# Three 64-byte steps in the SBUF layout of a two-model transformer kernel

## The chip, the core and the metric

The kernel runs on one core of a Trainium2 chip. The metric is the device time of one execution in microseconds (us). Within 0.5% is what a measurement of this kernel can hardly tell from no change.

## What is computed

A sequence of 256 positions with 1,024 features passes through two models of two layers each, all in float32. A layer of the first model is a feed-forward block, a mixer and a second feed-forward block, with a norm at the end:

```python
for l in range(DEPTH):
    x = x + 0.5 * swiglu_ffn(rmsnorm(x, ffn1_norm[l]), ffn1_w_up[l], ffn1_w_down[l])
    x = x + mixer(rmsnorm(x, mix_norm[l]), w_in[l], ...)
    x = x + 0.5 * swiglu_ffn(rmsnorm(x, ffn2_norm[l]), ffn2_w_up[l], ffn2_w_down[l])
    x = rmsnorm(x, final_norm[l])
```

The mixer projects its input to values, a gated convolution input, queries and keys, and gates; it runs dilated window attention and a convolution of 31 taps over the sequence, projects both, gates them, and projects the sum out. A layer of the second model has a mixer of a Fourier transform and windowed attention, and one feed-forward block with a convolution of three taps. The feed-forward width is 2,816 everywhere.

## The kernel before

**Precision in three products.** Every weight matrix is split into a high part (float32 rounded to the float32r format) and a low part, and so is every activation. A product is three matmuls into the same PSUM bank: high weights by high activations (L437), high weights by low activations (L438), low weights by high activations (L439). Each has 128 x 128 weights (stationary) and 256 columns of activations (moving). In the profile's names, `bank<-h_lo,hi` is a matmul whose moving operand is `h_lo` and whose weights are a tile of `hi`.

```python
    mm(out, w_hi, a_hi, start=start, stop=False, skip_group_check=True)
    mm(out, w_hi, a_lo, start=False, stop=False, skip_group_check=True)
    return mm(out, w_lo, a_hi, start=False, stop=True, skip_group_check=True)
```

**Weight stream.** Weights come in chunks of 128 x 2048 (16 tiles) into `raw`, which has three slots. SyncE issues the loads in the order of the program, ScalarE copies `raw` to `hi` (L1059), VectorE subtracts to get `lo` (L1570), and TensorE uses the chunk in 48 matmuls. All orders are written out by hand; no scheduler moves anything.

**Moving operands by stage.** The feed-forward blocks stream `n_hi` and `n_lo` (the scaled input) against the up weights, `hid_hi` and `hid_lo` against the down weights, and `last_hi` and `last_lo` in the last down chunk alone. The mixer of the first model streams `h_hi` and `h_lo`, its normed input, through 8 chunks of the gated convolution input (two tiles of 128 outputs by 8 tiles of features each), 12 chunks of queries and keys, and 8 chunks of gates; then `yt` and `s` through the projections of attention and convolution; then `h_hi` and `h_lo` again, which now hold the mix, through the output projection. The second model uses `n`, `f` and `g`, and `h` in its output projection. `x` and `sq` hold the residual and a scratch copy of it.

**Beside the matmuls.** In the stage of queries and keys VectorE also turns the heads (L1734, L1736), scales them (L1744) and works off the taps of the convolution (`cv`, L1771), a fixed number of taps behind each chunk.

**Layout.** `sb()` hands out SBUF addresses upward from `state["at"]`, rounded up to 64 bytes, except where an address is given; those are offsets from four marks (`at_m`, `at_a` with `at_v` and `at_u` above it, and `at_t`). The first address is 16,512. Byte addresses within a partition:

| tiles | address before | remainder by 128 |
|---|---|---|
| `raw`, `hi`, `lo` (slots of 8,192 bytes, tiles of 512) | 16,512; 41,088; 65,664 | 0 |
| `x`, `h_hi`, `h_lo`, `sq` (slices of 1,024) | 90,240; 98,432; 106,624; 114,816 | 0 |
| `const` and the masks | 123,008; 129,664 | 0 |
| `s_hi`, `f_hi`, `qk` (from `at_a`) | 144,704 | 64 |
| `hid_hi` (from `at_v`) | 169,280 | 64 |
| `n_hi`, `yt_hi`, `g_hi` (from `at_u`); `n_lo` | 181,568; 189,760 | 64 |
| `cv`, `gate` | 190,720; 198,912 | 0 |
| `zt`, `p_sb`, `sgm`, `last_hi` (from `at_t`) | 215,296 | 0 |

Of the kernel before, what the change touches and what calls it, by code (L numbers as in the profile page):

```python
# [233 lines left out]
def build(nc, d):  # L234
# [5 lines left out]
    state = {"at": -(-nc.sbuf_base // 64) * 64}  # L240

    def sb(name, shape, dt, at=None):
        size = int(np.prod(shape[1:])) * 4
        if at is None:
            at = state["at"]
            state["at"] += -(-size // 64) * 64
        return nc.alloc_sbuf_tensor_at(name, shape, dt, offset=at)

    raw = sb("raw", [P, SLOTS, CW], F32)
    hi = sb("hi", [P, SLOTS, CW], F32R)  # L250
    lo = sb("lo", [P, SLOTS, CW], F32R)
    x = sb("x", [P, KT, S], F32)
    h_hi = sb("h_hi", [P, KT, S], F32R)
    h_lo = sb("h_lo", [P, KT, S], F32R)
    sq = sb("sq", [P, KT, S], F32)
    const = sb("const", [P, C["mask1"]], F32)
    eps = const[:, C["eps"]:C["eps"] + 1]
    at_m = state["at"]
# [33 lines left out]
    gate = sb("gate", [P, 16, S], F32)  # L292
    bv = sb("bv", [P, GROUPS * 512], F32, at_u + (KT * UPW + KT * S) * 4)
    spread = sb("spread", [P, 2 * ROWS * HD], F32, at_u + (KT * UPW + KT * S) * 4 + 10240)
    at_t = state["at"]
    z = sb("z", [P, 2, S], F32)
    zsq = sb("zsq", [P, 2, S], F32)
# [2143 lines left out]
```

## Time and profile before

| | |
|---|---|
| median of the runs | 2016.39 us |
| lowest and highest of 3 | 2011.72 and 2020.76 us |
| profiled execution, its own time | 2009.35 us |
| span of its trace | 2007.5 us |
| TensorE busy | 1945.0 us (97%) |
| VectorE, ScalarE busy | 1493.7 us, 1078.1 us |
| mean granted TensorE clock | 0.992 |

Matmuls overlap in the pipeline: one has a duration of about 0.28 us in the trace, but the next starts about 0.12 us after it. So TensorE's pace is not read from durations or from the busy share, but from how many matmuls fit into a stretch in which it never stops. The rows of the trace stand below the change.

### The profile page before, as it was taken

Reading aid. Unit: us, or ns where it says so; the run is one execution under the profiler, and the core shown is the slowest. Engines: PE = TensorE matmul, PEld = TensorE weight load, DVE = VectorE, ACT = ScalarE, POOL = GpSimd, SP = SyncE. Lnnn points to the kernel's source line nnn. Section 1 sums busy time; section 2 is a strip of 40 time slices with the busy share of each in tenths; the row PEclk is TensorE's granted clock in tenths of the full one; section 3 lists DMA queues with packets and bytes.
Section 4 is the critical chain, followed back from the end, with each engine's and each line's share of the span. In section 5 each row is a group of like instructions: output and inputs, shape, how many; then the busy total and the mean of one; then the engine's idle time right before and its main releaser. Section 6 shows DMA issues by size and latency. Waiting matters only on the chain.

```text
span 2007.5 us, 39036 instructions
## 1 busy us (share of the span) xinstructions
PE 1945.0 (97%) x15906; PEld 1873.5 (93%) x15906; DVE 1493.7 (74%) x2183; ACT 1078.1 (54%) x1358; POOL 31.4 (2%) x40
## 2 busy tenths in 40 slices
PE   7999999999999999999998999999999999999998
PEld 6999999799999999999987999999889999889998
DVE  6555889987755576568899787555778777878776
ACT  5444566566544444445665765444565555565554
POOL 0000011000000000000100000000000000000000
PEclk9999999999999999999999999999999999999999
DMA  6555589534655445555985256554335554334553
GB/s 244 204 184 214 189 245 263 151 98 137 226 201 182 176 147 188 191 218 189 269 243 148 86 170 219 188 188 161 114 111 184 188 188 167 128 136 161 195 190 135
DMA packets 61001, 362.26 MB, mean 180 GB/s; under 512 B 7904, under 2 KB 8160, under 8 KB 24160
## 3 DMA queue, kind: packets, MB, share of 16 engines
q1 hardware_dynamic: 54704, 339.37, 47.9%
q0 software_dynamic: 5184, 18.88, 5.4%
q10 hardware_dynamic: 1008, 2.51, 0.3%
q8 instruction: 78, 1.28, 0.3%
q14 instruction: 27, 0.22, 0.0%
HBM read 353.39 MB, written 1.05 MB: 177 GB/s over the span
## 4 chain that ended last, share of the span: by engine, by line
PE 78%; DVE 15%; ACT 4%; DMA 2%; issue 1%; DVEq 0%; ACTq 0%; SPq 0%
PE bank L437 24%; PE bank L438 24%; PE bank L439 24%; DVE lo L1570 5%; DVE cv L1771 3%; ACT hi L1059 2%; DMA raw<-in_w 1%; DVE zt L1734 1%; PE bank L642 1%; DVE n_lo L1574 1%; PE bank L615 1%; PE bank L628 1%; DMA x<-in_x 1%; DVE qk L1744 1%; PE bank L600 0%
## 5 line engine op out<-in xcount | busy, mean ns | idle before, releaser
L1570 DVE TENSOR_TENSOR lo<-raw,hi 128x2048 fp32r<-128x2048 f32 (+1 forms) x336 | 676.5, 2014 | 216.6 <-ACT hi L1059 216.2
L437 PE MATMUL bank<-n_hi,hi 128*128 128x256 f32 x2256 | 637.3, 283 | 29.9 <-DVE lo L1798 12.6
L1059 ACT ACTIVATE hi<-raw 128x2048 fp32r<-128x2048 f32 (+1 forms) x336 | 598.3, 1783 | 105.1 <-PE bank L439 86.9
L438 PE MATMUL bank<-n_lo,hi 128*128 128x256 f32 x2256 | 631.1, 280 | 0.0
L439 PE MATMUL bank<-n_hi,lo 128*128 128x256 f32 x2256 | 631.0, 280 | 0.0
L437 PEld LDWEIGHTS bank<-n_hi,hi 128*128 128x128 f32 x2256 | 429.6, 190 | 36.0 <-DVE lo L1798 12.6
L438 PEld LDWEIGHTS bank<-n_lo,hi 128*128 128x128 f32 x2256 | 426.8, 189 | 1.2 <-issue 1.0
L439 PEld LDWEIGHTS bank<-n_hi,lo 128*128 128x128 f32 x2256 | 427.9, 190 | 0.0
L437 PE MATMUL bank<-h_hi,hi 128*128 128x256 f32 x1152 | 335.7, 291 | 4.8 <-DVE h_lo L1574 4.8
L438 PE MATMUL bank<-h_lo,hi 128*128 128x256 f32 x1152 | 326.9, 284 | 0.0
L439 PE MATMUL bank<-h_hi,lo 128*128 128x256 f32 x1152 | 326.6, 284 | 0.0
L437 PE MATMUL bank<-hid_hi,hi 128*128 128x256 f32 x960 | 267.6, 279 | 0.6 <-DVE lo L1570 0.6
L438 PE MATMUL bank<-hid_lo,hi 128*128 128x256 f32 x960 | 267.4, 279 | 0.0
L439 PE MATMUL bank<-hid_hi,lo 128*128 128x256 f32 x960 | 267.4, 279 | 0.0
L437 PEld LDWEIGHTS bank<-h_hi,hi 128*128 128x128 f32 x1152 | 221.6, 192 | 17.5 <-issue 12.5
L438 PEld LDWEIGHTS bank<-h_lo,hi 128*128 128x128 f32 x1152 | 221.9, 193 | 0.6
L439 PEld LDWEIGHTS bank<-h_hi,lo 128*128 128x128 f32 x1152 | 221.9, 193 | 0.0
L1108 ACT ACTIVATE silu_t<-up_t 128x256 f32<-128x256 f32 x88 | 36.8, 418 | 299.6 <-DVE up_t L1625 299.6
L1771 DVE SCALAR_TENSOR_TENSOR cv<-upad,prm,cv 128x256 f32<-128x256 f32 x480 | 195.2, 476 | 0.0
L437 PEld LDWEIGHTS bank<-hid_hi,hi 128*128 128x128 f32 x960 | 181.6, 189 | 1.0 <-DVE lo L1570 1.0
L439 PEld LDWEIGHTS bank<-hid_hi,lo 128*128 128x128 f32 x960 | 180.9, 188 | 0.0
L438 PEld LDWEIGHTS bank<-hid_lo,hi 128*128 128x128 f32 x960 | 180.2, 188 | 0.0
(243 smaller groups left out, 2291.5 us busy)
## 6 DMA issues: line engine op xcount, KB each, us to landing
raw<-in_w SPq DMA_DIRECT2D x286, 1024.0 KB, 4.8
raw<-in_w SPq DMA_DIRECT2D x53, 512.0 KB, 4.0
lo<-in_w POOLq DMA_DIRECT2D x36, 512.0 KB, 8.2
zt<-zt SPq DMA_DIRECT2D x96, 64.0 KB, 5.8
bv<-in_bv SPq DMA_DIRECT2D x2, 768.0 KB, 6.1
spread<-in_spread SPq DMA_DIRECT2D x2, 768.0 KB, 8.0
x<-in_x ACTq DMA_DIRECT2D x4, 256.0 KB, 10.3
out_x<-sq SPq DMA_DIRECT2D x1, 1024.0 KB, 3.9
```

Source lines behind the costliest of these rows:

```text
L437: mm(out, w_hi, a_hi, start=start, stop=False, skip_group_check=True)
L438: mm(out, w_hi, a_lo, start=False, stop=False, skip_group_check=True)
L439: return mm(out, w_lo, a_hi, start=False, stop=True, skip_group_check=True)
L615: last = mm(bank[3 + e][:, at:at + n], qk[r, 4 * g + hp, qt * P:(qt + 1) * P], qk[r, 12 + 4 * g + hp, cols], start=(g == 0), stop=True, sk ...
L628: last = nc.tensor.transpose(bank[5 + e][:, b * P:(b + 1) * P], p_sb[:, e, b * P:(b + 1) * P], ident)
L642: last = mm(bank[Y_BANK][e * HD:(e + 1) * HD, qt * P:(qt + 1) * P], v_sb[:, kt, v:v + HD], pt_sb[:, e, b, :], start=(b == 0), stop=(b == 3 ...
L1059: fn(hi[:, s, 0:w], raw[:, s, 0:w], ACT.Copy).then_inc(sem["hi"], 1)
L1108: fn(silu_t[:, u, :], gate_of[:, u, 0, :], ACT.Silu).then_inc(sem["silu"], 1)
L1570: v.tensor_tensor(lo[:, s, 0:w], raw[:, s, 0:w], hi[:, s, 0:w].bitcast(F32), ALU.subtract)\
L1574: return v.tensor_tensor(out, full, high.bitcast(F32), ALU.subtract).then_inc(sem[name], 1)
L1734: link(v.tensor_tensor(both, both, turns, ALU.mult))
L1771: ins = v.scalar_tensor_tensor(cv[:, t, :], src, w, cv[:, t, :], ALU.mult, ALU.add)
```

## The change

Three lines are added, each of which moves the mark from which the following tiles get their addresses by 64 bytes.

```diff
     lo = sb("lo", [P, SLOTS, CW], F32R)
+    state["at"] += 64
     x = sb("x", [P, KT, S], F32)
     h_hi = sb("h_hi", [P, KT, S], F32R)
     h_lo = sb("h_lo", [P, KT, S], F32R)
     sq = sb("sq", [P, KT, S], F32)
+    state["at"] += 64
     const = sb("const", [P, C["mask1"]], F32)
...
     spread = sb("spread", [P, 2 * ROWS * HD], F32, at_u + (KT * UPW + KT * S) * 4 + 10240)
+    state["at"] += 64
     at_t = state["at"]
     z = sb("z", [P, 2, S], F32)
```

`raw`, `hi` and `lo` keep their addresses. `x`, `h_hi`, `h_lo` and `sq` move up by 64 bytes, to 90,304 and so on, a remainder by 128 of 64 where it was 0. Everything from `const` to `spread` moves up by 128 bytes, so its remainder stays. `zt`, `p_sb`, `sgm`, `last_hi` and `last_lo` and what else stands behind `at_t` moves up by 192 bytes, to a remainder of 64 where it was 0. With the three lines in, the five engines have the same instructions in the same order, with the same shapes and the same waits; only base addresses differ.

## Rows read from the trace of the kernel before

**Rows 1.** The page: busy time by engine, and shares of the last-ending chain by engine.

```profile
PE 1945.0 (97%) x15906; PEld 1873.5 (93%) x15906; DVE 1493.7 (74%) x2183; ACT 1078.1 (54%) x1358; POOL 31.4 (2%) x40
PE 78%; DVE 15%; ACT 4%; DMA 2%; issue 1%; DVEq 0%; ACTq 0%; SPq 0%
```

**Rows 2.** Costliest groups by form: busy us, mean ns, by name of moving operand.

```profile
L438 PE MATMUL bank<-n_lo,hi 128*128 128x256 f32 x2256 | 631.1, 280 | 0.0
L438 PE MATMUL bank<-h_lo,hi 128*128 128x256 f32 x1152 | 326.9, 284 | 0.0
L438 PE MATMUL bank<-s_lo,hi 128*128 128x256 f32 x128 | 35.3, 276 | 0.0
L438 PE MATMUL bank<-last_lo,hi 128*128 128x256 f32 x96 | 28.6, 298 | 0.0
```

**Rows 3.** Stretches: length, each engine's busy time and instructions, clock, DMA.

```profile
core 0: us, PE busy (x) PEld busy (x) DVE busy (x) ACT busy (x) POOL busy (x), PEclk, DMA share, GB/s
229.00:277.00 48.00, 48.00 (x402) 48.00 (x402) 39.47 (x68) 24.01 (x21) 1.87 (x2) 1.00 0.62 195
473.00:493.00 20.00, 20.00 (x179) 20.00 (x178) 17.93 (x25) 10.76 (x14) 0.00 (x0) 1.00 0.62 202
27.00:197.00 170.00, 170.00 (x1446) 170.00 (x1445) 101.51 (x97) 73.54 (x76) 0.00 (x0) 1.00 0.56 200
728.00:892.00 164.00, 164.00 (x1449) 164.00 (x1449) 100.69 (x96) 73.41 (x75) 0.00 (x0) 1.00 0.56 202
1549.00:1690.00 141.00, 141.00 (x1246) 141.00 (x1246) 110.38 (x150) 80.73 (x97) 0.00 (x0) 1.00 0.54 191
199.00:204.00 5.00, 5.00 (x44) 5.00 (x43) 4.93 (x9) 3.78 (x5) 0.00 (x0) 1.00 0.40 129
894.00:899.00 5.00, 5.00 (x45) 5.00 (x44) 4.93 (x8) 3.15 (x4) 0.00 (x0) 1.00 0.33 92
```

**Rows 4.** Groups in 229:277 (h_lo) and 473:493 (s_lo): matmuls and weight loads.

```profile
L438 PE MATMUL bank<-h_lo,hi 128*128 128x256 f32 x134 | 37.9, 283 | 0.0
L438 PEld LDWEIGHTS bank<-h_lo,hi 128*128 128x128 f32 x134 | 25.7, 192 | 0.0
...
L438 PE MATMUL bank<-s_lo,hi 128*128 128x256 f32 x60 | 16.6, 276 | 0.0
L438 PEld LDWEIGHTS bank<-s_lo,hi 128*128 128x128 f32 x60 | 11.3, 188 | 0.0
```

**Rows 5.** Weight loads in 93:141, same columns as rows 4.

```profile
L439 PEld LDWEIGHTS bank<-n_hi,lo 128*128 128x128 f32 x92 | 17.7, 192 | 0.0
L437 PEld LDWEIGHTS bank<-n_hi,hi 128*128 128x128 f32 x91 | 17.1, 188 | 0.0
```

**Rows 6.** Matmuls of h_lo in 228:286, 286:319, 390:457 and 1490:1509.

```profile
L438 PE MATMUL bank<-h_lo,hi 128*128 128x256 f32 x160 | 45.3, 283 | 0.0
...
L438 PE MATMUL bank<-h_lo,hi 128*128 128x256 f32 x80 | 22.6, 283 | 0.0
...
L438 PE MATMUL bank<-h_lo,hi 128*128 128x256 f32 x98 | 28.0, 285 | 0.0
...
L438 PE MATMUL bank<-h_lo,hi 128*128 128x256 f32 x48 | 14.3, 298 | 0.0
```

**Rows 7.** Chain that ended last by line: 286:319, 319:370, 390:457, 493:519.

```profile
by line: PE bank L437 32.0%; PE bank L438 29.1%; PE bank L439 29.0%; PE bank L578 8.8%; ACT zt L1169 1.7%; issue 0.1%
...
by line: DVE cv L1771 34.2%; DVE lo L1570 20.0%; DVE zt L1734 15.7%; DVE qk L1744 7.7%; issue 6.2%; ACT hi L1059 3.5%; DVE rstd L1886 3.3%; DVE qk L1736 3.0%; ACT L1175 2.5%; ACT zgsq L1178 1.4%; DVE cv L1768 1.3%; ACT zt L1169 1.2%; ACT st
...
by line: PE bank L437 21.0%; PE bank L438 17.8%; PE bank L439 17.7%; PE bank L615 10.0%; PE bank L642 9.8%; PE bank L628 9.7%; PE bank L600 7.0%; PE bank L715 5.4%; ACT pt_sb L1197 1.6%; issue 0.1%
...
by line: DMA raw<-in_w 49.5%; DVE lo L1570 23.0%; ACT hi L1059 19.3%; issue 3.8%; DVE t L1968 3.1%; DVE sq L1971 2.7%; DVE h_lo L1574 2.7%; ACT h_hi L1326 2.5%; DVE sq L1604 2.4%; ACT xsq L1091 2.4%; DVE x L1642 2.3%; DVE t L1966 2.3%; PE b
```

**Rows 8.** Two more stretches, columns as in rows 3.

```profile
228.00:286.00 58.00, 58.00 (x484) 57.79 (x484) 48.27 (x85) 31.11 (x29) 3.60 (x4) 1.00 0.67 205
...
319.00:370.00 51.00, 49.62 (x351) 41.85 (x349) 49.21 (x83) 30.16 (x39) 4.32 (x5) 1.00 0.87 242
```

## The prediction

> **What bounds the kernel now.** First the page: TensorE is busy for 97% of the span and has 78% of the chain that ended last, VectorE 15% [rows 1]. So the pace of the matmul stream is the time, except where VectorE or the weight stream holds it up. Second the costliest groups: matmuls of one shape, one instruction and one kind of weights, have four mean durations, by the name of the moving operand: 276 ns with `s_lo`, 280 with `n_lo`, 284 with `h_lo`, 298 with `last_lo` [rows 2]. The last two are the operands whose remainder by 128 equals that of the weights in `hi` and `lo`; `s` and `n` stand at 64.
>
> Third the pace itself, from stretches in which TensorE never stops. A stretch also counts the matmuls that reach over its edges, so I divide its length plus one duration by its count. From 229 to 277 us, all `h`: (48,000 + 283) / 402 = 120.1 ns from start to start. From 473 to 493, all `s`: (20,000 + 276) / 179 = 113.3 ns. The feed-forward blocks (`n` and `hid`) have two paces. From 27 to 197: 170,281 / 1446 = 117.8 ns; from 728 to 892: 164,276 / 1449 = 113.4 ns; from 1549 to 1690: 141,276 / 1246 = 113.4 ns [rows 3]. Of the six blocks three are like the first (the stretches 529:699 and 1222:1392 have the same count) and three like the others (1845:1986 too). These are the same chunks of code at the same addresses, so a block falls into one of two paces, and keeps it to its end. `last` has 5,281 / 44 = 120.0 ns in one block and 5,281 / 45 = 117.4 ns in another [rows 3]; this count is coarse.
>
> Fourth, what is longer in the slow pace. With `s` a matmul has 276 ns and its neighbouring weight load 188; with `h` 283 and 192 [rows 4]. In a slow feed-forward block one of the three loads, that of the low tile, has 192 ns and the others 188 [rows 5]. I read this as two readers of SBUF that meet: the stream of moving columns and the load of the next tile. With equal remainders they meet at every matmul; 64 bytes apart they meet never or in part, by how the two happen to be placed in time when the stream starts. The durations show that both wait; that the remainder by 128 is what counts is my inference from which names are slow. `last`, whose address has the weights' remainder by 128 but not by 256 (0 against 128), is slow as well, so a remainder by 256 fits worse.
>
> **The change part by part.** No instruction is added, removed or reordered.
>
> *First step: `h` from remainder 0 to 64.* The `h` stream then stands to the weights as `n`, `hid`, `s` and `yt` do now. Its pace goes from 120.1 to 113.3 (6.8 ns less) or to 117.8 (2.3 ns less). By the six feed-forward blocks the chance is one half each; the `s` stretch is fast, and so I take 60% fast: 0.6 x 6.8 + 0.4 x 2.3 = 5.0 ns per matmul.
>
> Which `h` matmuls count? Each row of the groups by stretch stands for one of the three products, so times three. In 228:286 (gated convolution input and the first two chunks of queries and keys) 160 x 3 = 480; TensorE never stops there, VectorE is busy for 48.27 of 58 us and so has some 9.7 us to come forward [rows 6, 8]. In 286:319 80 x 3 = 240, and the chain runs through TensorE [rows 6, 7]. In 319:370 the chain is VectorE's: taps 34.2%, `lo` 20.0%, turning 15.7% [rows 7], with VectorE busy for 49.21 of 51 us [rows 8]; a faster matmul there buys nothing of its own, but the stage starts earlier by what was won before, since VectorE's idle time ahead of it is larger than the 720 x 6.8 = 4.9 us that it could be at most. In 390:457 (gates) 98 x 3 = 294 on a chain of TensorE [rows 6, 7]. In 493:519 (output projection) the chain goes through the weight loads (49.5%), `lo` and `hi` [rows 7]: its 192 matmuls count for 0, at most 192 x 6.8 = 1.3 us. That is 480 + 240 + 294 = 1,014 per layer, 2,028 for both. The output projection of the second model has 48 x 3 = 144 in 1490:1509 [rows 6], 288 for its two layers. Sum 2,316 x 5.0 ns = 11.6 us. Bounds: all slow 2,316 x 2.3 = 5.3 us; all fast 2,316 x 6.8 = 15.7, with the two output projections 18.4 us.
>
> *Third step: `last` from 0 to 64.* Six blocks of 48 make 288 matmuls. From a mean of (120.0 + 117.4) / 2 = 118.7 to 0.6 x 113.3 + 0.4 x 117.8 = 115.1 is 3.6 ns: 1.0 us, between 0 and 288 x 6.8 = 2.0.
>
> *`x`, `sq`, `zt`, `p_sb` and `sgm` at other remainders.* These are VectorE's, ScalarE's and the transfers'. The trace doesn't show them at other addresses. VectorE's nearest rows are the 51 us of 319:370, where turning has 15.7% of the chain [rows 7]: 1% either way on those 8 us is 0.1 us per layer. I take 0, and keep 0.5 us either way.
>
> *Second step: `n`, `hid`, `s` and the rest by 128 bytes.* Their remainder by 128 stays. I take 0. If the remainder counts by 256 after all, their relation to the weights changes from 64 below to 64 above. A gain from it can't exceed what the three slow blocks would give, (170,281 - 1446 x 113.4) ns = 6.3 us each; the loss is the rival below.
>
> Sum: 11.6 + 1.0 = 12.6 us. The profiled execution took 2009.35 us, so its like comes to 1996.8 us. The median of the runs shown is 2016.39, which is 7.0 us above it: about the price of one feed-forward block more in the slow pace. Against it the forecast is 2016.4 - 12.6 = 2003.8, **2004 us**.
>
> **A rule that speaks against it.** The rows show a matmul 7 ns and its weight load 4 ns longer with `h` than with `s` [rows 4]. The Trainium skill, "TensorE: Matmul & The Clock Gate", section "Step-by-step: what each phase is for", says that TensorE has two independent read ports of SBUF, one for the moving operand and one for the weights, and that "Loading the next tile's weights doesn't steal SBUF read bandwidth from the running matmul". By that rule the addresses cannot matter to the matmuls and the sum would be 0, 2016.4 us. The trace does not agree with it for the pace of `h`; what it leaves open is whether the address is the cause.
>
> **The rivals.**
> *No effect* (chance 0.12): the pace of `h` has another cause than its address. For it: between the stages chunk lengths, PSUM banks and VectorE's load differ too. Against it: `h` has 283 to 285 ns in three stages that differ in just these ways [rows 6]. It gives 2016 us. This is also the case that the change doesn't do what it should.
> *Always the partial meeting* (0.18): `h` falls into the pace of 117.8 ns. Then 5.3 us and little from `last`: 2011 us.
> *The feed-forward blocks go slow* (0.12, the other side): the move by 128 bytes, or the other arrival times at a block's start, put the fast blocks into the pace of 117.8 ns. The price is 4.4 ns a matmul, 1449 x 4.4 = 6.4 us for the block at 728 and 1246 x 4.4 = 5.5 us for each of the two late ones [rows 3], together 17.4 us. For it: which pace a block gets is decided at its start by times that this change moves. Against it: three of six are fast now, and nothing in their own addresses by 128 changes. With `h` in the slow pace as well it gives 2016.4 + 17.4 - 5.3 = 2028.5 us. It decides when more than two blocks flip and none flips back, since two cost 11.9 us and the forecast gains 12.6.
> *The forecast* (0.58).
>
> **How the numbers follow.** The forecast's own range is 18.4 + 2.0 = 20.4 us at most and 5.3 at least, so 1996 to 2011; a feed-forward block that falls out otherwise moves either end by 6.3. The range for 8 in 10 leaves out a block flipped on top of an all-fast case below, and most of the slow rival above: 1993 to 2017, which takes in no effect. What counts as faster is under 2006.3, which needs 10.1 us of the 12.6: the forecast and hardly any rival, 0.57. Within 0.5%, up to 2026.5: no effect, the partial meeting and single flips, 0.33. Slower: 0.10.
>
> **What would show it.** Right: the same stretch of `h` has about 425 matmuls in 48 us instead of 402, with 276 and 188 ns, or about 410 with 281; the stage of queries and keys is as long as before between its VectorE instructions but starts 1.5 to 5 us earlier; `last` falls below 281 ns in its unstalled middle. Wrong: `h` still at 283 and 192 ns (the address is not it), or `n` and `hid` at a third pace (the 128 bytes matter). The total is wrong with the mechanism right if the number of slow feed-forward blocks is not three, since one is worth half of the whole gain.

## The result and the profile after

The changed kernel has a median of 2020.53 us (20 runs, 2008.95 to 2026.47); the kernel before, run beside it, 2015.63 us (20 runs, 2009.52 to 2020.76). The ratio is 1.0024, 95% interval 1.0013 to 1.0034: about 4.9 us slower (2.6 to 6.9). The forecast was 2004 and its range ended at 2017. The profiled execution after took 2020.89 us, with a span of 2019.1 us; the one before took 2009.35 us.

First the page after, with the busy time by engine and the chain that ended last, as in [rows 1]. Three lines are added above them, so L437, L438 and L439 of before are L440, L441 and L442 here.

```profile
PE 1958.1 (97%) x15906; PEld 1886.1 (93%) x15906; DVE 1494.3 (74%) x2183; ACT 1079.0 (53%) x1358; POOL 31.4 (2%) x40
...
PE 79%; DVE 15%; ACT 3%; DMA 1%; issue 1%; DVEq 0%; ACTq 0%; SPq 0%
```

TensorE has 13 us more of busy time and the other engines have what they had: a change of pace in the main, not a new wait. The groups by form, as in [rows 2]:

```profile
L441 PE MATMUL bank<-n_lo,hi 128*128 128x256 f32 x2256 | 633.5, 281 | 0.0
...
L441 PE MATMUL bank<-h_lo,hi 128*128 128x256 f32 x1152 | 322.4, 280 | 0.0
...
L441 PE MATMUL bank<-s_lo,hi 128*128 128x256 f32 x128 | 35.7, 279 | 0.0
...
L441 PE MATMUL bank<-last_lo,hi 128*128 128x256 f32 x96 | 27.4, 285 | 0.0
```

`h_lo` fell from 284 to 280 ns and `last_lo` from 298 to 285, as meant. But `s_lo` rose from 276 to 279, and `n_lo` from 280 to 281, over 2,256 instructions. The pace shows more. The same stretches as in [rows 3], with their columns:

```profile
229.00:277.00 48.00, 48.00 (x410) 48.00 (x409) 40.12 (x69) 24.66 (x22) 1.88 (x2) 1.00 0.62 198
473.00:493.00 20.00, 20.00 (x172) 20.00 (x171) 18.06 (x26) 8.51 (x10) 0.00 (x0) 1.00 0.63 199
27.00:197.00 170.00, 170.00 (x1445) 170.00 (x1445) 101.51 (x97) 73.61 (x75) 0.00 (x0) 1.00 0.56 201
728.00:892.00 164.00, 164.00 (x1395) 164.00 (x1394) 97.27 (x90) 70.38 (x71) 0.00 (x0) 1.00 0.55 195
1549.00:1690.00 141.00, 141.00 (x1200) 141.00 (x1199) 107.52 (x146) 78.51 (x94) 0.00 (x0) 1.00 0.53 191
199.00:204.00 5.00, 5.00 (x45) 5.00 (x44) 4.93 (x9) 3.80 (x5) 0.00 (x0) 1.00 0.46 149
...
1500.00:1512.00 12.00, 12.00 (x108) 12.00 (x108) 10.11 (x16) 5.35 (x7) 0.00 (x0) 1.00 0.63 215
```

With (length + one duration) / count: `h` has 48,280 / 410 = 117.8 ns (120.1 before). `s` has 20,279 / 172 = 117.9 (113.3 before). The first feed-forward block has 117.8 as before, but the stretches of the third and the fifth have 164,281 / 1395 = 117.8 and 141,281 / 1200 = 117.7, where they had 113.4. `last` has 45 in its 5 us in the first block, where it had 44. So the two paces that the prediction read are both still there, but after the change all six feed-forward blocks, `yt`, `s` and the long stretches of `h` in the first model are in the slower one. The faster one is left in a few single chunks of `h` and in one of the two output projections of the second model (the last row, `h` at the same address: 12,276 / 108 = 113.7).

The matmuls of `h` in 229:277, as in [rows 4], with one of the three weight loads (the other two have 188 and 187 ns):

```profile
L441 PE MATMUL bank<-h_lo,hi 128*128 128x256 f32 x137 | 38.4, 280 | 0.0
...
L440 PEld LDWEIGHTS bank<-h_hi,hi 128*128 128x128 f32 x137 | 25.8, 188 | 0.0
```

The load fell from 192 to 188 ns and the matmul from 283 to 280. The weights did not move, so the duration of their load goes by the place of the moving operand. The pace is that of the partial meeting, but the durations are different from those that the prediction read for it: in the slow blocks of the kernel before one of the three loads has 192 ns and the matmuls have 281 [rows 5], while here no load has more than 188 and the matmuls have 279 or 280.

What `h` gained is seen in when the next stage starts. The matmuls of `yt_hi` (64 instructions, shortest/median/longest duration in ns, first and last start in us) in a second profile of the kernel before, and in the changed kernel:

```profile
L437 PE MATMUL bank<-yt_hi,hi x64: 276/276/473, 459.8 to 1169.8; 128*128 128x256 f32 x64
...
L440 PE MATMUL bank<-yt_hi,hi x64: 280/280/470, 457.6 to 1167.4; 128*128 128x256 f32 x64
```

The stage of `yt` starts 2.2 us earlier and runs with 280 ns instead of 276. Counted from the first matmul of `h`, which starts at 228.3 us here and at 227.8 there, it comes after 229.3 us; so it does in a second profile of the changed kernel. In three profiles with `h` at 0 (the two of before, and e1 below) it comes after 232.0 to 233.0: 2.7 to 3.7 us are won in the first layer. In the second layer it comes after 229.9 and 231.2 us, against 230.6 to 232.1, about 1 us. By its last start 2.4 us are left of this in the profile shown, and in the second profile of the changed kernel (1170.4) nothing: `yt` and `s` have given back a part, and the rest differs from one execution to the next.

The chain by line in 319:370, as in [rows 7], is still VectorE's, with turning at 15.7% in both: the new addresses of `zt`, `p_sb` and `sgm` cost nothing that this view shows. Ahead of it, in 286:319, the chain was TensorE's before [rows 7]; in the changed kernel, the second line below, it is now that of the turning of the heads (its transfer into `zt`, and VectorE).

```profile
by line: DVE cv L1774 41.2%; DVE lo L1573 19.8%; DVE zt L1737 15.7%; DVE qk L1747 7.7%; issue 5.4%; DVE qk L1739 4.3%; PE bank L618 3.6%; DVE rstd L1889 3.3%; DVE cv L1771 1.3%; DVEq L1744 0.0%
...
by line: DMA zt<-zt 31.9%; DVE cv L1774 21.6%; DVE zt L1737 10.7%; DVE lo L1573 6.9%; PE bank L442 5.6%; PE bank L440 5.1%; PE bank L441 5.1%; SPq L374 5.1%; DVE qk L1739 4.2%; ACT zt L1172 3.1%; issue 0.7%
```

### The profile page after: what moved, and what is told of

It is laid out like the page before. It is cut to its first block, busy times and chain, and to the rows that moved or that the text cites. A ratio compares the mean times of both kernels' runs of the same rounds, so it can differ in the third digit from the quotient of the medians.

```text
span 2019.1 us, 39036 instructions
## 1 busy us (share of the span) xinstructions
PE 1958.1 (97%) x15906; PEld 1886.1 (93%) x15906; DVE 1494.3 (74%) x2183; ACT 1079.0 (53%) x1358; POOL 31.4 (2%) x40
## 4 chain that ended last, share of the span: by engine, by line
PE 79%; DVE 15%; ACT 3%; DMA 1%; issue 1%; DVEq 0%; ACTq 0%; SPq 0%
PE bank L440 25%; PE bank L441 24%; PE bank L442 24%; DVE lo L1573 4%; DVE cv L1774 3%; ACT hi L1062 2%; DVE zt L1737 1%; PE bank L618 1%; PE bank L645 1%; DVE n_lo L1577 1%; PE bank L631 1%; DMA x<-in_x 1%; DMA zt<-zt 1%; DVE qk L1747 1%; DVE sq L1607 0%
## 5 line engine op out<-in xcount | busy, mean ns | idle before, releaser
L440 PE MATMUL bank<-n_hi,hi 128*128 128x256 f32 x2256 | 639.2, 283 | 29.7 <-DVE lo L1801 12.5
L442 PE MATMUL bank<-n_hi,lo 128*128 128x256 f32 x2256 | 633.5, 281 | 0.0
L441 PE MATMUL bank<-n_lo,hi 128*128 128x256 f32 x2256 | 633.5, 281 | 0.0
L440 PEld LDWEIGHTS bank<-n_hi,hi 128*128 128x128 f32 x2256 | 426.6, 189 | 35.5 <-DVE lo L1801 12.5
L441 PEld LDWEIGHTS bank<-n_lo,hi 128*128 128x128 f32 x2256 | 427.2, 189 | 1.2 <-issue 1.0
L442 PEld LDWEIGHTS bank<-n_hi,lo 128*128 128x128 f32 x2256 | 426.6, 189 | 0.0
L440 PE MATMUL bank<-h_hi,hi 128*128 128x256 f32 x1152 | 331.2, 288 | 4.1 <-DVE h_lo L1577 3.9
L441 PE MATMUL bank<-h_lo,hi 128*128 128x256 f32 x1152 | 322.4, 280 | 0.0
L442 PE MATMUL bank<-h_hi,lo 128*128 128x256 f32 x1152 | 322.0, 280 | 0.0
L440 PE MATMUL bank<-hid_hi,hi 128*128 128x256 f32 x960 | 268.2, 279 | 0.3 <-DVE lo L1573 0.3
L442 PE MATMUL bank<-hid_hi,lo 128*128 128x256 f32 x960 | 268.3, 279 | 0.0
L441 PE MATMUL bank<-hid_lo,hi 128*128 128x256 f32 x960 | 268.2, 279 | 0.0
L440 PEld LDWEIGHTS bank<-h_hi,hi 128*128 128x128 f32 x1152 | 217.2, 189 | 16.9 <-issue 13.8
L441 PEld LDWEIGHTS bank<-h_lo,hi 128*128 128x128 f32 x1152 | 217.2, 189 | 0.5
L442 PEld LDWEIGHTS bank<-h_hi,lo 128*128 128x128 f32 x1152 | 217.3, 189 | 0.0
L440 PEld LDWEIGHTS bank<-hid_hi,hi 128*128 128x128 f32 x960 | 180.0, 187 | 0.8 <-DVE lo L1573 0.8
L441 PEld LDWEIGHTS bank<-hid_lo,hi 128*128 128x128 f32 x960 | 180.2, 188 | 0.0
L442 PEld LDWEIGHTS bank<-hid_hi,lo 128*128 128x128 f32 x960 | 180.0, 188 | 0.0
```

## The experiments

In the prediction the remainder by 128 bytes of a moving operand decided how it meets the weights. By the result a rival theory is due: **by 256** (A), in which 64 above the weights and 64 below them (192 above) are different places. Its rival is **history** (B): the address counts by 128 only, and what a stage draws depends on when, and behind what, its stream starts. The table has for each kernel the bytes added ahead of `x`, `const` and `at_t`, and where the moving operands then stand above the weights by 256.

| kernel | added | `h` | `n` `hid` `s` `yt` | `last` | median (runs) | before beside it | ratio [95%] |
|---|---|---|---|---|---|---|---|
| before | 0/0/0 | 0 | 192 | 128 | | | |
| after | 64/64/64 | 64 | 64 | 64 | 2020.53 (20) | 2015.63 | 1.0024 [1.0013, 1.0034] |
| e1 | 0/128/0 | 0 | 64 | 0 | 2026.25 (5) | 2015.69 | 1.0056 [1.0037, 1.0074] |
| e2 | 64/192/0 | 64 | 192 | 128 | 2012.34 (10) | 2015.69 | 0.9991 [0.9977, 1.0004] |
| e3 | 192/64/0 | 192 | 192 | 128 | 2007.29 (10) | 2015.69 | 0.9962 [0.9946, 0.9978] |
| e4 | 32/0/0 | 32 | 224 | 160 | 2029.55 (4) | 2015.69 | 1.0070 [1.0050, 1.0091] |
| e5 | 224/0/0 | 224 | 160 | 96 | 2032.74 (8) | 2013.25 | 1.0089 [1.0062, 1.0116] |
| e6 | 96/0/0 | 96 | 32 | 224 | 2019.53 (8) | 2013.25 | 1.0024 [0.9999, 1.0049] |
| e7 | 64/0/0 | 64 | 0 | 192 | 2043.75 (2) | 2013.25 | 1.0115 [1.0061, 1.0170] |
| e9 | 192/64/64 | 192 | 192 | 192 | 2005.37 (7) | 2016.88 | 0.9941 [0.9921, 0.9961] |
| e12, as e9 | 192/64/64 | 192 | 192 | 192 | 2009.03 (10) | 2015.72 | 0.9972 [0.9947, 0.9998] |
| e10 | 32/64/64 | 32 | 32 | 32 | 2013.87 (10) | 2016.88 | 0.9981 [0.9966, 0.9996] |

All rows below are stretches with the columns of [rows 3] in which TensorE never stops (in 474:490 of e12 the weight loads pause for 0.12 us). 231:279 is `h` in the gated convolution input, 474:490 is `s`, and 60:190, 560:690, 760:890, 1260:1390, 1570:1680 and 1870:1980 lie in the six feed-forward blocks. In 48 us a pace of 120 ns has 402 matmuls, 117.8 ns has 410 and 113.4 ns has 425; in 130 us they are 1086, 1106 and 1149; in 110 us the last two are 936 and 973; in 16 us 138 and 144.

**The second step alone (e1).**

```diff
     sq = sb("sq", [P, KT, S], F32)
+    state["at"] += 128
     const = sb("const", [P, C["mask1"]], F32)
```

> x, h_hi, h_lo and sq stay at their old addresses; everything from const on moves up by 128 bytes. By 256, h then stands at 0 to the weights and n, hid, s, yt at 64 above them, where before they were 64 below; last stands at 0. Theory A (the remainder by 256 counts: 64 above is the slow pace, 64 below either): h stays at 120.1 ns, but s, yt and all six feed-forward blocks run at 117.8 ns, as in the changed kernel; the time is 1 to 1.01 of before (about +15 us against the profiled execution). Theory B (what streamed before counts: the h stream at remainder 0 sets what follows into the fast pace): s and yt at 113.3 ns, three or so of six blocks fast, and a time as before.

```profile
231.00:279.00 48.00, 48.00 (x402) 48.00 (x402) 40.09 (x71) 23.05 (x21) 2.33 (x3) 1.00 0.67 211
474.00:490.00 16.00, 16.00 (x138) 16.00 (x137) 14.34 (x20) 8.09 (x9) 0.00 (x0) 1.00 0.66 198
...
1570.00:1680.00 110.00, 110.00 (x936) 110.00 (x935) 80.11 (x111) 58.40 (x70) 0.00 (x0) 1.00 0.53 189
1870.00:1980.00 110.00, 110.00 (x973) 110.00 (x973) 84.61 (x115) 61.87 (x75) 0.00 (x0) 1.00 0.54 191
```

The ratio gives 11.3 us more (7.5 to 14.9). `h` stays at 402, as its address does. `s` has 138 and block 5 has 936, where both were fast, and only block 6 draws the fast pace. This is A: 128 bytes, which leave every remainder by 128 alone, cost more than the whole change. The line moves `last` and VectorE's tiles behind `const` too, but the loss is seen in the pace of `s` and of a late block, in stretches where TensorE never stops.

**`h` moved by 64, the rest by 256 (e2), and `h` by 192, the rest by 256 (e3).** In both, `n`, `hid`, `s` and `yt` keep their place above the weights.

```diff
     lo = sb("lo", [P, SLOTS, CW], F32R)
+    state["at"] += 64
...
     sq = sb("sq", [P, KT, S], F32)
+    state["at"] += 192
```

> x, h_hi, h_lo and sq move up by 64 bytes and everything from const on by 256, so that n, hid, s, yt keep their remainder by 256 (64 below the weights) and h stands 64 above. Theory A: h mostly 117.8 ns as in the changed kernel, s and yt and about half of the feed-forward blocks at 113.3, last as before near 119; 8 us less than before. Theory B (there is no stream at remainder 0 left ahead of s): s, yt and all blocks at 117.8 ns, 5 us more than before.

```profile
231.00:279.00 48.00, 48.00 (x410) 48.00 (x409) 41.15 (x73) 23.43 (x21) 2.73 (x3) 1.00 0.68 216
474.00:490.00 16.00, 16.00 (x139) 16.00 (x138) 14.70 (x21) 7.99 (x9) 0.00 (x0) 1.00 0.62 198
...
1570.00:1680.00 110.00, 110.00 (x937) 110.00 (x936) 81.47 (x110) 59.67 (x72) 0.00 (x0) 1.00 0.51 176
1870.00:1980.00 110.00, 110.00 (x973) 110.00 (x972) 86.71 (x115) 62.28 (x75) 0.00 (x0) 1.00 0.53 188
...
1178.00:1194.00 16.00, 16.00 (x138) 16.00 (x137) 13.96 (x20) 7.09 (x8) 0.00 (x0) 1.00 0.58 179
```

`h` has the 410 of the changed kernel. The ratio gives -1.8 us (-4.6 to +0.8), so the loss of e1 is gone when the rest stays at 192. But `s` has 139, the slow pace, at the place where it was fast before, in the second layer too (the last row, where `s` in e3 has 143), and one late block is slow. That is not in A; it is what B says. The same edit with 192 and 64 is e3:

> x, h_hi, h_lo and sq move up by 192 bytes and everything from const on by 256: h, n, hid, s and yt all stand 64 below the weights by 256. Theory A: h at 113.3 in part of its stages, the blocks half fast as before; 8 to 15 us less than before. Theory B: as the changed kernel, nearly all at 117.8 ns and 5 us more than before, since nothing at remainder 0 is left.

```profile
231.00:279.00 48.00, 48.00 (x410) 48.00 (x409) 41.20 (x74) 23.38 (x22) 2.73 (x3) 1.00 0.67 217
474.00:490.00 16.00, 16.00 (x144) 16.00 (x143) 14.48 (x21) 8.05 (x9) 0.00 (x0) 1.00 0.63 198
...
1570.00:1680.00 110.00, 110.00 (x973) 110.00 (x972) 87.54 (x117) 62.58 (x76) 0.00 (x0) 1.00 0.55 193
```

`h` has 410 here as well, `s` 144 and block 5 973. The ratio gives -7.7 us (-10.9 to -4.4), the first version that is faster than both kernels.

**The other places (e4 to e7).** Each has one line more, ahead of `x`, with 32, 224, 96 and 64 bytes, which moves everything behind the weights alike:

```diff
     lo = sb("lo", [P, SLOTS, CW], F32R)
+    state["at"] += 32
     x = sb("x", [P, KT, S], F32)
```

> Everything from x on moves up by 32 bytes: h stands 32 above the weights by 128, n, hid, s and yt 96, last 32. If two readers meet in units of 64 bytes, half of each unit now meets, and both families run between 113.3 and 120.1 ns, in a pace of their own. If only equal remainders meet, h falls to 113.3 or 117.8 ns and n stays as it is. If both families get a pace under 113.3, the fast pace has a cost left that an offset takes away.

```profile
231.00:279.00 48.00, 48.00 (x414) 48.00 (x413) 41.37 (x72) 24.14 (x21) 2.53 (x3) 1.00 0.66 210
...
60.00:190.00 130.00, 130.00 (x1101) 130.00 (x1101) 75.00 (x70) 53.42 (x53) 0.00 (x0) 1.00 0.57 202
```

`h` at 32 has 48,280 / 414 = 116.6 ns, a third pace; `n` at 224 has 130,281 / 1101 = 118.3 ns, in all six blocks. The ratio gives 14 us more (10 to 18), and the four runs lie within 2.9 us.

> Everything from x on moves up by 224 bytes. Above the weights by 256, h stands at 224, n, hid, s and yt at 160, last at 96. So far h at 0 has 120.1 ns, h at 32 has 116.7, n and h at 64 have 117.8, last at 128 some 119, last at 160 some 117.5, n at 192 has 113.4 or 117.8, n at 224 has 118.3. If the pace depends on the remainder by 256 alone, h at 224 runs at 118.3 as n did, and n at 160 near 117.5. If it depends on the remainder by 128 alone, h at 224 (96 by 128) has 118.3 and n at 160 (32 by 128) has 116.7.

```profile
231.00:279.00 48.00, 48.00 (x408) 48.00 (x407) 40.72 (x73) 23.07 (x21) 2.73 (x3) 1.00 0.67 217
...
60.00:190.00 130.00, 130.00 (x1110) 130.00 (x1109) 75.34 (x70) 54.08 (x55) 0.00 (x0) 1.00 0.58 204
```

`h` at 224 has 408, or 118.3 ns, the pace that `n` had there: in these two cases the pace goes by the place and not by the operand or its stage. `n` at 160 has 117.4 ns here and 110,280 / 930 = 118.6 in the second model.

> Everything from x on moves up by 96 bytes: h at 96, n, hid, s and yt at 32, last at 224. If the remainder decides and not the tile, n at 32 runs at 116.7 ns as h did, always, without two paces, and the feed-forward blocks together cost about as much as in the kernel before; h at 96 is new: 118.3 if the remainder by 128 is all that counts.

```profile
231.00:279.00 48.00, 48.00 (x402) 48.00 (x402) 40.11 (x73) 22.27 (x20) 2.74 (x3) 1.00 0.68 219
...
60.00:190.00 130.00, 130.00 (x1117) 130.00 (x1116) 75.22 (x70) 54.89 (x55) 0.00 (x0) 1.00 0.57 206
```

`n` at 32 has 130,280 / 1117 = 116.6 ns, again the pace of `h` at that place, and `h` at 96 has 402, the count of the equal place.

> Everything from x on moves up by 64 bytes: n, hid, s and yt now stand at 0 to the weights, h at 64, last at 192. If the equal remainder is what made h slow, n, hid, s and yt run at 120 ns: some 9,300 of their matmuls lose 4.5 ns each against the mean of the profiled execution before, 42 us, and h gains 2.3 ns x 2,316 = 5 us: about 2047 us. If h was slow for another reason, n keeps its pace and the time falls by 5 us.

```profile
231.00:279.00 48.00, 48.00 (x410) 48.00 (x409) 40.08 (x69) 24.95 (x21) 1.88 (x2) 1.00 0.61 195
...
60.00:190.00 130.00, 130.00 (x1086) 130.00 (x1085) 73.65 (x68) 52.96 (x53) 0.00 (x0) 1.00 0.56 199
```

With `n` at the weights' own place the blocks have 1086: 130,283 / 1086 = 120.0 ns, the pace of `h` in the kernel before. The kernel takes 2043.75 us, the slowest of all, near the 2047 that were expected if the equal place is what makes `h` slow. It has two runs only, and the ratio of the medians would be 1.0151. `h` stands at 64 and has 410.

**The two kernels again (e8, e11), each unchanged, one profile.**

> The kernel before once more, for a second profile. If a feed-forward block's pace is drawn at its start in each execution, other blocks than in the first profile are at 113.4 and 117.8 ns; the h stages stay at 120.1 ns. If the pace is fixed by the program, it is again the third, fifth and sixth block that are fast.

```profile
760.00:890.00 130.00, 130.00 (x1106) 130.00 (x1105) 74.27 (x70) 54.67 (x55) 0.00 (x0) 1.00 0.56 199
...
1570.00:1680.00 110.00, 110.00 (x973) 110.00 (x973) 85.06 (x114) 62.99 (x75) 0.00 (x0) 1.00 0.54 188
1870.00:1980.00 110.00, 110.00 (x973) 110.00 (x973) 87.57 (x117) 62.29 (x75) 0.00 (x0) 1.00 0.55 191
...
1701.30:1709.70 8.40, 8.35 (x48) 8.38 (x49) 5.32 (x11) 4.49 (x6) 0.00 (x0) 0.65 0.21 62
```

2013.73 us. Block 3 has 1106 now, where it had 1149: the kernel before had three fast blocks in one execution and two in the other, and blocks 5 and 6 are fast in both. The last row is `last` in block 5: its 48 matmuls need 8.4 us at a granted clock of 0.65, where they lie in 7.5 us at 0.77 in the first profile (1699:1706.5). In block 6 it is again 8.4 us at 0.65.

> The changed kernel once more, for a second profile. If 64 above the weights makes the slow pace the usual one, again at most one of the six feed-forward blocks is at 113.4 ns, and h, s and yt are at 117.8 but for single chunks. If the first profile was chance, two to four blocks are fast.

```profile
760.00:890.00 130.00, 130.00 (x1106) 130.00 (x1106) 75.03 (x70) 53.92 (x55) 0.00 (x0) 1.00 0.56 198
...
1570.00:1680.00 110.00, 110.00 (x937) 110.00 (x936) 80.11 (x110) 58.68 (x70) 0.00 (x0) 1.00 0.53 189
1870.00:1980.00 110.00, 110.00 (x937) 110.00 (x936) 80.12 (x110) 58.94 (x71) 0.00 (x0) 1.00 0.54 190
```

2023.62 us, and no block is fast again.

**All moving operands at 192 (e9, e12), and all at 32 (e10).**

```diff
     lo = sb("lo", [P, SLOTS, CW], F32R)
+    state["at"] += 192
...
     sq = sb("sq", [P, KT, S], F32)
+    state["at"] += 64
...
+    state["at"] += 64
     at_t = state["at"]
```

> h, n, hid, s, yt and last all stand 192 above the weights by 256 (64 below): x and its neighbours up by 192 bytes, everything from const on by 256, what lies behind at_t by 320. If the remainder by 256 sets the choice of paces, this is the experiment with h at 192 and last at 128 plus 288 x (119 - 114) ns = 1.4 us: about 8.5 us less than before, with runs spread over some 13 us since each block still draws between 113.3 and 117.8. If last has no such gain, it is the same time as there.

The profiled execution of e9 took 2021.41 us, far above the other six, which lie between 2001.48 and 2008.29. Its stretches, the last one of `h` in the second layer:

```profile
231.00:279.00 48.00, 48.00 (x410) 48.00 (x409) 41.14 (x73) 23.36 (x21) 2.74 (x3) 1.00 0.68 217
...
1570.00:1680.00 110.00, 110.00 (x936) 110.00 (x935) 80.27 (x109) 60.03 (x72) 0.00 (x0) 1.00 0.51 181
```

```profile
935.00:959.00 24.00, 24.00 (x214) 24.00 (x213) 20.76 (x35) 11.13 (x10) 0.00 (x0) 1.00 0.61 222
```

`h` draws 410 in one layer and 24,279 / 214 = 113.5 ns in the other, at one address and in one execution; no feed-forward block is fast. So the median was not explained by this profile, and the same kernel was run once more:

> The kernel with all moving operands at remainder 192 once more, because its profiled execution (2021.41 us) was far above its other runs (2001.48 to 2008.29) and showed no feed-forward block in the fast pace. Theory: remainder 192 lets a block draw between 117.8 and 113.4 ns, and this kernel's usual run has three to five of six blocks fast. Then the median is 2003 to 2009 us again, and a profiled execution of 2001 to 2009 us has at least three stretches with 1149 matmuls in 130 us (or 973 in 110 us); one near 2021 us has none. Rival: the gain of the median lies elsewhere (in h and in the projections) and the feed-forward blocks stay at 1106 and 936; then an execution near 2005 us shows none or one fast block and the h stretch at 425 in 48 us.

```profile
231.00:279.00 48.00, 48.00 (x425) 48.00 (x425) 42.66 (x77) 25.13 (x26) 2.74 (x3) 1.00 0.70 221
...
60.00:190.00 130.00, 130.00 (x1106) 130.00 (x1105) 75.30 (x70) 53.64 (x54) 0.00 (x0) 1.00 0.57 203
...
1570.00:1680.00 110.00, 110.00 (x973) 110.00 (x973) 86.24 (x114) 62.37 (x76) 0.00 (x0) 1.00 0.53 187
1870.00:1980.00 110.00, 110.00 (x973) 110.00 (x972) 84.59 (x115) 61.29 (x73) 0.00 (x0) 1.00 0.55 194
```

```profile
935.00:959.00 24.00, 24.00 (x214) 24.00 (x213) 20.89 (x39) 10.68 (x10) 0.00 (x0) 1.00 0.57 202
```

This execution took 2005.92 us. `h` has 425 and 214, the fast pace in both layers; blocks 5 and 6 have 973, and blocks 1 to 4 the slow count. The expected three fast blocks were wrong. Nor does the fast `h` bring what it should: the first matmul of `yt` starts at 457.1 us, against 457.6 in the changed kernel with 117.8 ns and 459.8 in the kernel before. The chain by line in 228:286 goes some way to show why, and below it stand the stretches behind (columns as in [rows 3]):

```profile
by line: PE bank L440 25.1%; PE bank L442 24.8%; PE bank L441 24.7%; DMA lo<-in_w 18.3%; ACT hi L1062 3.3%; ACT lo L1066 1.9%; issue 1.3%; PE bank L581 1.0%; ACT sgm L1260 0.0%
```

```profile
319.00:370.00 51.00, 46.30 (x326) 38.22 (x324) 50.50 (x85) 27.22 (x34) 4.31 (x5) 0.97 0.86 247
370.00:390.00 20.00, 18.01 (x138) 16.94 (x137) 19.16 (x45) 12.61 (x20) 0.86 (x1) 0.90 0.26 56
```

In 228:286 18.3% of the chain is now the transfer of the weights, where before and in the changed kernel it is TensorE's alone; in 286:319 it is the turning of the heads, as in the changed kernel. In 319:370 TensorE is busy for 46.30 us where it had 49.62 [rows 8], and the granted clock is 0.90 in 370:390. TensorE does its matmuls sooner, and waits. Against the second profile of before this execution is 7.8 us shorter; 3.1 us of it are won by the last matmul of `yt` (1169.8 before). In the second model the two output projections of `h` are fast, some 1 us each, and `last` in block 5 needs 5.7 us at full clock (1700:1705.7) and not 8.4 at 0.65; other stages give a part of this back.

The second set of runs gives a smaller gain than the first, -5.6 us against -11.9 us; taken together they are no clear step beyond e3.

> h, n, hid, s, yt and last all stand 32 above the weights. With a pace fixed by the remainder, every family runs at 116.7 ns in every block: against the experiment with n at 32 and h at 96 (2019.5 us) h gains (119.9 - 116.7) x 2316 = 7.5 us, about 2012 us, 3 us less than before, and the runs lie within 4 us of each other, since no block draws. If the time is that of before or the runs spread over 10 us, the pace is not fixed by the remainder.

```profile
231.00:279.00 48.00, 48.00 (x413) 48.00 (x413) 41.36 (x76) 23.56 (x23) 2.74 (x3) 1.00 0.69 221
474.00:490.00 16.00, 16.00 (x140) 16.00 (x139) 14.27 (x21) 6.99 (x8) 0.00 (x0) 1.00 0.64 197
60.00:190.00 130.00, 130.00 (x1117) 130.00 (x1116) 75.34 (x70) 54.78 (x55) 0.00 (x0) 1.00 0.58 206
```

All blocks have 116.7 ns (the others 1116 or 1117, and 945 in 110 us), `h` 413 and `s` 140. The ratio gives -3.8 us (-6.9 to -0.8), and the ten runs lie within 6.0 us, where the sixteen of the kernel before span 14.6.

## Why the prediction was wrong

**The second step is the one that failed.** The prediction took "I take 0" for `n`, `hid`, `s` and the rest by 128 bytes. Alone it costs 11.3 us (e1, which also puts `last` at 0). Two things led there. That the remainder by 128 counts was inferred from which names are slow, with only two remainders in sight. And `last` at 128 above the weights was slow like `h` at 0, from which the text said that "a remainder by 256 fits worse". But two slow places out of eight say nothing against eight different ones: by 256, 0 and 128 are both slow (120.0 and 118.5 to 120.0 ns), and 64 and 192 differ only in how often they draw the fast pace.

**First step: mechanism right, size off.** The address does decide the pace of `h`, so the rival of no effect fell, and with it what the prediction took from the Trainium skill's rule in "TensorE: Matmul & The Clock Gate", section "Step-by-step: what each phase is for", as far as it speaks of these float32r matmuls: moving `n` to the weights' own place put it from 117.8 to 120.0 ns a matmul (e7). The term was 2,316 x 5.0 = 11.6 us on the assumption that `h` is fast 60% of the time. At 64 it seldom was: in four profiles (after, after again, e2, e7) the stretch in the first layer has 409 or 410 in 48 us, a few single chunks are fast, and of the eight output projections in the second model two. The term is then about 2,316 x 2.3 = 5.3 us, the bound "all slow". Of its two parts in the first model, 1,014 x 2.3 = 2.3 us each, the starts of `yt` show 2.7 to 3.7 us in the first layer and about 1 in the second. Even luck would not have brought the rest: with `h` at 113.4 ns in both layers (e12) `yt` comes 229.0 and 231.5 us after the first matmul of `h`. That is 3 to 4 us less than with `h` at 0 in the first layer and no less in the second, where 1,014 x 6.8 = 6.9 were expected in each. The prediction checked that VectorE had room in 228:286; it didn't see that the turning is the limit in 286:319 already at 117.8 ns, nor that the weight transfers come into the chain of 228:286 at 113.4.

**Third step: 0.4 us instead of 1.0.** By the first and last start of its 48 matmuls `last` has 120.0 and 118.7 ns in the first and third block of the kernel before, at 128, and 117.7 and 117.9 in the changed kernel, at 64: 288 x 1.5 ns.

**The sum by the medians, on two paths.** The ratio of after less that of e1 is 0.0032, or 6.4 us, for steps one and three together with the rest at 64 (give or take 4 us by the two intervals); their terms now make 5.3 + 0.4 = 5.7. On the other path the terms don't come out: e2 is the first step with the rest left at its place, and it gives 1.8 us, at most 4.6, and not 5.3. Its profile shows where a part went. `yt` and `s`, which in e2 keep their place above the weights, were slow in both layers: 32 x 3 and 64 x 3 matmuls by 4.5 ns, 1.3 us a layer, and 5.3 - 2.6 = 2.7 lies inside the interval. In the changed kernel they lose the same, which the prediction had not priced either. So the steps do not simply add up: the second costs 11.3 us with `h` at 0, and with `h` at 64 (the ratio of after less that of e2, 0.0033, which has the third step in it) 6.7.

What happened is two rivals at once, each of which was priced: the partial meeting and the blocks that go slow, which together gave 2028.5 with three blocks. That it was less would fit a usual execution of before with two fast blocks and not three, as in its second profile; its first, of 2009.35 us, lay 6.3 us below the median. Two profiles make this likely and no more.

**VectorE's terms: 0, as taken.** Turning has 15.7% of the chain in 319:370 before and after.

**The draw is the part that stays open.** Fast feed-forward blocks at 192 were, in six profiles (before, before again, e2, e3, e9, e12), 1 of 24 in the first model and 9 of 12 in the second; at 64, in three profiles (after, after again, e1), 0 of 12 and 1 of 6. The late blocks of one execution mostly fall alike (both fast in four of these nine profiles, both slow in three), so these counts alone are thin. What shows that the place by 256 matters for `n`, `hid`, `s` and `yt` is the medians: before against e1, and e2 against after, whose intervals don't overlap although after has `last` at the better place. What decides the single draw is open. `yt` and `s` at 192 were fast in both layers of five profiles and slow in both layers of e2 alone, where `h` ran ahead of them at 64: this fits B as a second influence, but one execution can't settle it. No run tried to change when a stream starts.

**A rival that no run tested.** Every experiment moved the moving operands, and `raw`, `hi` and `lo` stayed at their addresses. So the runs can't tell the place above the weights from the operand's own address by 256 (at place 0 that is 128). That the unmoved weights take 192 ns to load with `h` at 0 and 188 with `h` at 64 speaks for two readers that meet; a run with the weights moved instead would show it.

## What to carry to other kernels

Where a kernel is bound by TensorE with a weight load for every matmul, the place of each moving operand above the weight tiles by 256 bytes is a setting of its own (whether moving the weights instead does the same is not shown): step it in 32 bytes and read the pace by counting matmuls in stretches without a stall, for every stage, since a line that moves one tile moves all tiles behind it too. A conclusion on which remainder counts needs more places than the kernel happens to have; one more kernel that moves a single group, as e1 did, would have cost less than the reasoning. And where identical stretches have two paces within one execution, price a change from many timed runs, and look at two profiles before a pace is taken for the kernel's own.

## What the runs showed of the hardware

Pace of a float32r matmul with 128 x 128 weights, its own weight load and 256 moving columns, at full clock, by the bytes that the moving operand stands above the weights by 256 (`last` by the first and last start of its 48 matmuls in blocks 1 and 3):

| place | ns from start to start | seen in |
|---|---|---|
| 0 | 120.0 | `h` before, e1; `n` e7; `last` e1 |
| 32 | 116.7 | `h` e4, e10; `n` e6, e10; `last` e10 |
| 64 | 117.8, seldom 113.3 | `h` after, e2, e7 (two output projections fast); `n` after, e1 (one block fast); `last` after |
| 96 | 120.0 | `h` e6; `last` e5 |
| 128 | 118.5 to 120.0 | `last` before, e2, e3 |
| 160 | 117.4 or 118.6 | `n` e5; `last` e4 (117.4) |
| 192 | 117.8 or 113.4 | `n` before, e2, e3, e9, e12; `h` e3, e9, e12; `last` e7, e9, e12 |
| 224 | 118.3 | `n` e4; `h` e5; `last` e6 |

Between the best and the worst place lie 6.7 ns in 113.3, or 6%, and in the kernel's time 1.5% (ratios 0.9962 of e3 to 1.0115 of e7; 1.9% by their medians). At 64 and 192 the same code at the same addresses has two paces, and a stretch of 110 or 130 us holds one of them from end to end. The slow pace is the same at both places and its durations are not: at 192 one of every three weight loads has 192 ns and the matmuls 281 (which of the three differs from block to block: in e3 that of the low tile in 60:190, that of `n_hi` and the high tile in 560:690), at 64 no load has more than 188 and the matmuls 279 or 280. The fast pace has 276 and 188 at both, and at 0 all three loads have 192 and the matmuls 283.

Where all operands stand at 32, which showed one pace only, the spread of ten runs is 6.0 us. That a block's pace is drawn anew in each execution is a likely source of the spread of 8 to 18 us that sets of runs of the kernel before have: its two profiles differ by 4.4 us, with one block of some 6 us between them. It is hardly the only one. The clock that `last` is granted in blocks 5 and 6 moves each of these stages by 1 to 3 us, and the changed kernel spreads by 17.5 us, though its two profiles show no fast block.
